# A tuned two-block kernel: lighter pair loop, reordered late units and an interleaved seam to the first FFN

## The reference

```python
h = rms_norm(x, pre_g)
conv_in, z_c, u_s, z_s, g_c, g_s = split(h @ w_in)
cu = ca * sigmoid(cb)                      # conv_in = (ca, cb)
cu = silu(layer_norm(causal_depthwise_conv(cu, conv_w, conv_b)))   # 31 taps
conv_out = (cu * silu(z_c)) @ w_conv_out
y = gelu(s5_mimo(u_s, ...))                # 32 groups, complex state of 64, scan over time
y = y * sigmoid(y @ w_glu + b_glu)
ssm_out = (y * silu(z_s)) @ w_ssm_out
merged = sigmoid(g_c) * conv_out + sigmoid(g_s) * ssm_out
x = x + rms_norm(merged @ w_out, post_g)
```

## Time and profile before

| | us |
|---|---|
| median of 3 runs (2633.86 to 2638.43) | 2634.6 |
| the profiled execution | 2629.72 |
| its span, first to last instruction | 2627.9 |

### The profile page before, as it was taken

One profiled execution on the slowest core, in us unless ns is written; L12 is line 12 of the kernel. 1 busy time (PEld: TensorE's weight loads), 2 busy tenths in 40 slices (PEclk: granted clock), 3 DMA queues, 4 the chain that ended last, 5 costly groups with the idle time before them and its releaser, 6 DMA issues.

```text
span 2627.9 us, 36163 instructions
## 1 busy us (share of the span) xinstructions
PE 2536.4 (97%) x13941; PEld 1951.4 (74%) x13941; DVE 1269.8 (48%) x1578; ACT 853.8 (32%) x1152; POOL 1197.5 (46%) x601
## 2 busy tenths in 40 slices
PE   8999999899999999888999999999999999999999
PEld 7666668678888776876788887888887446788887
DVE  7999775543322478566433322333225665433301
ACT  5422253432222335233322223322223233322221
POOL 4799834444444446212444444444443201444443
PEclk9999999899999999999999999999999999999999
DMA  5222213233333322002333333333333211333332
GB/s 147 73 72 67 72 55 112 64 96 94 90 90 96 104 81 61 20 3 66 91 96 89 90 96 93 95 96 90 90 96 87 59 33 33 92 92 96 94 91 80
DMA packets 417608, 212.85 MB, mean 81 GB/s; under 512 B 16774, under 2 KB 415932, under 8 KB 417500
## 3 DMA queue, kind: packets, MB, share of 16 engines
q1 hardware_dynamic: 414475, 209.05, 27.5%
q10 hardware_dynamic: 3024, 2.30, 0.4%
HBM read 209.22 MB, written 2.10 MB: 80 GB/s over the span
## 4 chain that ended last, share of the span: by engine, by line
PE 85%; POOL 7%; DVE 5%; ACT 1%; issue 1%; DMA 0%; ACTq 0%; POOLq 0%; DVEq 0%
PE bank L339 22%; PE bank L336 22%; PE bank L332 22%; PE bank L1314 3%; POOL w_lo L312 2%; PE bank L1316 2%; PE bank L1315 2%; PE bank L2097 2%; PE bank L2659 1%; PE bank L2658 1%; PE bank L2701 1%; PE bank L2617 1%; POOL tmp L767 1%; POOL tmp L772 1%; POOL tmp L761 1%
## 5 line engine op out<-in xcount | busy, mean ns | idle before, releaser
L312 POOL TENSOR_TENSOR w_lo<-w_raw,w_hi 128x1024 fp32r<-128x1024 f32 (+3 forms) x420 | 979.3, 2332 | 1316.7 <-ACT w_hi L303 1314.9
L303 ACT ACTIVATE w_hi<-w_raw 128x1024 fp32r<-128x1024 f32 (+3 forms) x420 | 424.8, 1012 | 1395.6 <-PE bank L339 1208.3
L332 PE MATMUL bank<-hH,w_hi 128*128 128x512 f32 x1728 | 451.7, 402 | 18.3 <-ACT w_hi L303 8.9
L336 PE MATMUL bank<-hL,w_hi 128*128 128x512 f32 x1728 | 440.9, 396 | 1.6 <-DVE hL L358 1.6
L339 PE MATMUL bank<-hH,w_lo 128*128 128x512 f32 x1728 | 438.0, 395 | 0.0
L332 PEld LDWEIGHTS bank<-hH,w_hi 128*128 128x128 f32 x1728 | 326.0, 189 | 110.6 <-ACT w_hi L303 11.4
L336 PEld LDWEIGHTS bank<-hL,w_hi 128*128 128x128 f32 x1728 | 325.3, 188 | 83.1 <-DVE hL L358 3.8
L339 PEld LDWEIGHTS bank<-hH,w_lo 128*128 128x128 f32 x1728 | 323.9, 187 | 79.1
L504 DVE TENSOR_TENSOR tmp<-bank,R 128x512 f32<-128x512 f32 x88 | 60.8, 691 | 400.4 <-PE bank L339 400.2
L510 DVE TENSOR_TENSOR ffn_aL<-tmp,ffn_aH 128x512 f32 (+1 forms) x88 | 156.0, 1773 | 86.2 <-ACT ffn_aH L473 86.2
L336 PE MATMUL bank<-ffn_aL,w_hi 128*128 128x512 f32 x704 | 179.8, 395 | 0.0
(11 more groups left out here) (482 smaller groups left out, 2755.5 us busy)
## 6 DMA issues: line engine op xcount, KB each, us to landing
w_raw<-in_ffn_w_gate SPq DMA_DIRECT2D x88, 512.0 KB, 3.8
w_raw<-in_ffn_w_up SPq DMA_DIRECT2D x88, 512.0 KB, 3.8
w_raw<-in_ffn_w_down SPq DMA_DIRECT2D x64, 512.0 KB, 3.7
w_raw<-in_w_in SPq DMA_DIRECT2D x48, 512.0 KB, 3.8
w_raw<-in_even_w_in SPq DMA_DIRECT2D x26, 512.0 KB, 3.8
w_raw<-in_ffn_w_down SPq DMA_DIRECT2D x32, 384.0 KB, 3.2
w_raw<-in_w_conv_out SPq DMA_DIRECT2D x8, 512.0 KB, 3.6
w_raw<-in_w_out SPq DMA_DIRECT2D x8, 512.0 KB, 3.6
```

Of the source, the lines that this page charges most:

```text
L303: nc.scalar.activation(w_hi[u % 2][:, 0:K, :], w_raw[u % 4][:, 0:K, :], ACT.Identity).then_inc(w_hi_ready, 1)
L312: nc.gpsimd.tensor_tensor(w_lo[u % 2][:, 0:K, :], w_raw[u % 4][:, 0:K, :], w_hi[u % 2][:, 0:K, :].bitcast(F32), ALU.subtract).then_inc(w_l ...
L332: nc.tensor.matmul(out, H[:, k, :], sH[:, k0 + k, :], start=start and k == 0, stop=False)
L336: nc.tensor.matmul(out, H[:, k, :], sL[:, k0 + k, :], start=False, stop=False)
```

## The change

Its diff, cut to what it does:

- `phases` on GpSimd makes only `ph_sin`; `tables` on ScalarE takes `Abs` of it, its sine, and as cosine the sine of a quarter turn less the absolute value. The memory for `ph_cos` and `quarter` goes.
- The loop has 11 taps per pair instead of 12; 16 more come after it. Every pair has 2 units; `LATE_UNITS` has 6. Four late units come ahead of `cs(14)`, two behind it.
- `y_rest` of all tiles comes behind the last tap; the gate units use banks 6 and 7 instead of 2 and 3, with waits that fit.
- `first_unit` has the order of `unit`: high pass (waits for `w_hi`), low pass, then the pass of `w_lo` (waits for it only there).
- GpSimd's subtraction for the second FFN unit waits for the diagonal tiles. VectorE adds tile 7 too, and its `hL` steps come behind all scalings and additions.
- The first FFN begins with `first_two`: units 0 and 1 share each slice as it comes. Unit 2 follows, then the norm's product, then unit 3. ScalarE converts unit 2's weights ahead of its last square.

```diff
@@ order of units @@
-                mine = [gates.pop(0) for _ in range(3 if i >= PAIRS - 2 else 2)]
+                mine = [gates.pop(0) for _ in range(2)]
...
-        LATE_UNITS = list(range(len(ROLE), len(ROLE) + 4))
-        ROLE += gates[:4]
+        LATE_UNITS = list(range(len(ROLE), len(ROLE) + 6))
+        ROLE += gates[:6]
@@ first FFN, TensorE @@
+        def first_two(pe, u, q):
...
+            for k in range(DT):
+                pe.wait_ge(h_hi, DT * q + k + 1)
+                for c in range(2):
+                    nc.tensor.matmul(bank_of(u + c)[:, :], w_hi[(u + c) % 2][:, k, :], hH[:, k, :], start=k == 0, stop=False)
+            for k in range(DT):
+                pe.wait_ge(h_lo, DT * q + k + 1)
+                for c in range(2):
+                    nc.tensor.matmul(bank_of(u + c)[:, :], w_hi[(u + c) % 2][:, k, :], hL[:, k, :], start=False, stop=False)
+            for c in range(2):
+                pe.wait_ge(w_lo_ready, u + c + 1)
+                for k in range(DT):
+                    ins = nc.tensor.matmul(bank_of(u + c)[:, :], w_lo[(u + c) % 2][:, k, :], hH[:, k, :], start=False, stop=k == DT - 1)
+                ins.then_inc(unit_done, 1)
...
-            for c in range(2):
+            if e == 0:
+                first_two(pe, U, q)
+            for c in range(0 if e else 2, 2):
                 unit(pe, U + c, 8, hH, hL, ready=(h_lo, DT * q) if c == 0 else None)
+            if e == 0:
+                unit(pe, U + 2, 8, hH, hL)
             norm_pe(pe)
-            for c in range(2, 4):
+            for c in range(2 if e else 3, 4):
@@ first FFN, ScalarE @@
                 for j in range(DT):
+                    if j == 7:
+                        split_hi(act, U + 2)
...
-                split_hi(act, u + 2, it, 4)
+                if not (first and e == 0):
+                    split_hi(act, u + 2, it, 4)
@@ block 1, GpSimd @@
-                g.tensor_tensor(ph_cos[p_][:, :], ph_sin[p_][:, :], quarter[:, 0:1].to_broadcast([P, T]), ALU.add).then_inc(ph_ready, 1)
...
-                if len(PAIR_UNITS[i]) > 2:
-                    split_lo(pool, u0 + 3)
...
-            for n_ in range(U_GLU, U_F[0] + (2 if STOP > U_F[0] else 0)):
+            for n_ in range(LATE_UNITS[4], U_F[0] + (1 if STOP > U_F[0] else 0)):
                 split_lo(pool, n_)
+            pool.wait_ge(ln_gated, DIAG + TT)
+            if STOP > U_F[0]:
+                split_lo(pool, U_F[0] + 1)
@@ block 1, ScalarE @@
+                s.activation(cosT[p_][:, :], ph_sin[p_][:, :], ACT.Abs, scale=TURN_TO_RAD / TURN).then_inc(act_step, 1)
+                turned = act_sent(act_step)
                 s.activation(sinT[p_][:, :], ph_sin[p_][:, :], ACT.Sin, scale=TURN_TO_RAD / TURN).then_inc(tab_ready, 1)
-                s.activation(cosT[p_][:, :], ph_cos[p_][:, :], ACT.Sin, scale=TURN_TO_RAD / TURN).then_inc(tab_ready, 1)
+                act.wait_ge(act_step, turned)
+                s.activation(cosT[p_][:, :], cosT[p_][:, :], ACT.Sin, scale=-1.0, bias=QUARTER).then_inc(tab_ready, 1)
...
-            y_split(3, gelu(3))
             after_unit(LATE_UNITS[2])
             after_unit(LATE_UNITS[3])
+            y_split(3, gelu(3))
+            after_unit(LATE_UNITS[4])
+            after_unit(LATE_UNITS[5])
@@ block 1, VectorE @@
-        X_BY_DVE = (1, 3, 6)
+        X_BY_DVE = (1, 3, 6, 7)
...
-                taps(3)
+                taps(2)
...
-            taps(16)
-            for j in range(3):
-                y_rest(j)
+            taps(28)
             y_out(3)
             taps(len(TAP_ORDER) - taps_sent[0])
-            y_rest(3)
+            for j in range(4):
+                y_rest(j)
...
+            for j in range(DT):
+                o_scale(j)
+                if j in X_BY_DVE:
+                    x_add(j)
+            for j in range(DT):
                 norm_lo(j)
@@ block 1, TensorE @@
-                pe.wait_ge(w_lo_ready, u + 1)
+                pe.wait_ge(w_hi_ready, u + 1)
                 H, L = w_hi[u % 2], w_lo[u % 2]
                 for k in range(K):
                     if ready:
+                        pe.wait_ge(h1_hi if ready[0] is h1_lo else y_hi, ready[1] + k + 1)
+                    mm(out[:, :], H[:, k, :], sH[:, k, :], start=k == 0, stop=False)
+                for k in range(K):
+                    if ready:
                         pe.wait_ge(ready[0], ready[1] + k + 1)
-                    mm(out[:, :], H[:, k, :], sH[:, k, :], start=k == 0, stop=False)
                     mm(out[:, :], H[:, k, :], sL[:, k, :], start=False, stop=False)
+                pe.wait_ge(w_lo_ready, u + 1)
+                for k in range(K):
                     ins = mm(out[:, :], L[:, k, :], sH[:, k, :], start=False, stop=k == K - 1)
...
             w_in_unit(LATE_UNITS[0])
-            w_in_unit(LATE_UNITS[1])
+            for c in range(1, 4):
+                w_in_unit(LATE_UNITS[c])
             cs(PAIRS - 2)
-            w_in_unit(LATE_UNITS[2])
-            w_in_unit(LATE_UNITS[3])
+            w_in_unit(LATE_UNITS[4])
+            w_in_unit(LATE_UNITS[5])
```

More of the change, by code:

```diff
@@ L593, in build @@
         ph_sin = [b.put(f"ph_sin{i}", [P, T], I32) for i in range(3)]
-        ph_cos = [b.put(f"ph_cos{i}", [P, T], I32) for i in range(3)]
         b = Map(tab_at)
@@ L954, in first_act @@
             silu(0)
-            silu(1)
             after_unit(U_GC)
-            for j in range(2, 5):
+            for j in range(1, 5):
                 silu(j)
@@ L2841, in constants @@
     small[:, 4] = np.where(i % 64 < 32, -1.0, 1.0)
+    small[:, 5] = np.pi / 2
     s, t = i[:, None], i[None, :]
```

38 lines of the change are left out of this document (14 added, 24 removed).

## The result

The changed kernel takes 2613.4 us (median of 4 runs, 2608.2 to 2613.95), the kernel before 2634.2 us in the runs beside it (4 runs, 2632.92 to 2638.43). The ratio is 0.9914, with a 95% interval of 0.9903 to 0.9926: 20.8 us faster. The predicted number was 2610.6 us, range 2605.5 to 2620. The sign, the range and most terms held; the number is 2.8 us too low, and that small difference hides two larger ones, which this part takes apart.

A forecast was written before the change was run, and what follows sets the result against it. TensorE, busy 97% of the span, was held by waits and slow clock, GpSimd setting the pair loop's 14.84 us period. Terms summed to 24.0 us: 2629.7 to 2605.7 profiled, plus 4.9 to the median, 2610.6 us; range 2605.5 to 2620.

The forecast's parts named there:

- loop (pair 3 to the end of its units): Pair loop: waits 15.0, two slow stretches 3.4 and refills 1.5 go, less 0.5 for lag; gain 19.4 us.
- unit 0 in the new order: Kernel start: all high products run first, so unit 0 ends at 22.9 instead of 21.5 us; cost 1.4 us.
- input product of pair 0 (`Abs` ahead of the `u_s` copies): At tables(0): `Abs` delays the `u_s` copies in ScalarE's queue; cost 0 to 0.63, taken as 0.5 us.
- last state product: Behind the pair loop: the 2.7 us wait for `s_im` and 1.5 us of clock loss go; gain 4.2 us.
- `w_ssm_out`, output product's first unit: Late block 1: 1.0 us gained as the wait for `w_lo` goes; 1.0 us lost waiting for high tile and `mL`.
- seam, up to the fifth unit's end: Block 1's end into the first FFN: fifth unit starts at 536.0 instead of 538.36 us; gain 2.3 us.
- cover of 3.7 us: Pair loop: the new order asks for `w_lo` 3.7 us later, covering GpSimd's lag of some 3 us by pair 15.
- Rival A: Pair loop: GpSimd stays the bound and slow stretches move; total gain near 16 us, 2618.5 us; chance 0.21.
- both slow stretches go: Pair loop: without waits the two stretches at 0.83 clock, 1.7 us each, vanish; gain 3.4 us.
- Rival D: Phase-to-table ring becomes the loop's bound if `Abs` adds table loads; slower, 2641 us at 15.5 us per pair; chance 0.03.
- Rival C: Behind the loop: deferred taps and `y_rest` hold the column means, 7 us go; 2617.5 us; chance 0.08.
- The first diagonal: End of block 1: the diagonal tile no longer runs beside GpSimd's subtraction, falling from 1632 to under 300 ns; gain 1.36 us.

The follow-up runs named there:

- after_again: The changed kernel, unchanged, run and profiled a second time; 2612.4 us, ratio 0.9916.
- fifth_early: The changed kernel with ScalarE converting the fifth FFN unit's weights right behind the norm's root; 2607.8 us, ratio 0.99.
- old_seam: The changed kernel with the seam between block 1 and the first FFN as in the kernel before; 2614.9 us, ratio 0.9925.
- best_mix: fifth_early plus slice-by-slice order in unit 0 and the output product's first unit, and last `u_s` copies ahead of the next weights; 2601.9 us, ratio 0.9875.
- both shifted ones: after_shift1 and after_shift2, the changed kernel with added norm products ahead of the second block's mixer; 2611.0 and 2614.5 us.
- twelve_taps: The changed kernel with 12 taps per pair again and 12 instead of 28 between loop and `y_out(3)`; 2616.3 us, ratio 0.9926.
- order_only: The kernel before with only the new product order in `first_unit`; 2633.5 us, ratio 0.9995.
- before_again: The kernel before, unchanged, run and profiled a second time; 2635.1 us (one run).
- one_phase: The kernel before with only the lighter phase step: one GpSimd phase product per pair, `Abs` on ScalarE; 2620.75 us, ratio 0.9954.
- before_shift1: The kernel before with the norm's product ahead of the second block's mixer done three times, 0.9 us added; 2639.1 us (one run).
- after_shift1: The changed kernel with the norm's product ahead of the second block's mixer done three times, 0.9 us added; 2611.0 us (one run).
- after_shift2: The changed kernel with the norm's product ahead of the second block's mixer done five times, 1.8 us added; 2614.5 us (one run).

## Why the prediction was right, and where it was off

The terms against the milestones of the table:

| term | forecast | measured |
|---|---|---|
| loop (pair 3 to the end of its units) | 19.4 | 19.5 |
| unit 0 in the new order | -1.4 | -1.5 |
| input product of pair 0 (`Abs` ahead of the `u_s` copies) | -0.5 | -0.3 |
| pair 0 to pair 3, net, with the slow stretch from 70 us | not foreseen | -1.2 |
| last state product | 4.2 | 4.25 |
| `w_ssm_out`, output product's first unit | 1.0 - 1.0 | 0.2 |
| seam, up to the fifth unit's end | 2.3 | about 2.0 |
| sum up to 560 us | 24.0 | 23 |
| stage of small products | 0 | -7.9 (3 of it luck of before) |

**Loop.** The bound was read rightly. The two needs worked out from before's rows were 13.72 (GpSimd) and 13.5 (TensorE), and TensorE's pair came out at 13.56. GpSimd's own step, pair by pair, is its phase product:

```profile
109.16 1.04 POOL L775 TENSOR_TENSOR ph_sin<-tidx,phase 128x512 int32<-128x512 int32 x1
...
273.81 1.04 POOL L775 TENSOR_TENSOR ph_sin<-tidx,phase 128x512 int32<-128x512 int32 x1
```

These are 12 pairs, (273.81 - 109.16) / 12 = 13.72 us each, just the need that was worked out. So GpSimd is still the slowest of the three and falls behind TensorE by 0.16 us per pair; over 16 pairs that is 2.6 us, which the later demand for `w_lo` covers, as argued: no wait but one of 0.3 us in 80 to 305 us. By this estimate the cover of 3.7 us would not last in a loop of twice the pairs. The group of all its phase steps:

```profile
L775 POOL TENSOR_TENSOR ph_sin<-tidx,phase 128x512 int32<-128x512 int32 x14 | 14.6, 1042 | 1.1
```

One product of 1.04 us remains, the second, of the earlier trace rows, is gone. Rival A (2618.5 us) falls with this.

**The clock in the loop.** The choice that both slow stretches go, worth 3.4 us, was right here: none of the kernels with the changed loop shows one between 80 and 340 us (after, after_again, fifth_early, old_seam, best_mix, both shifted ones, and twelve_taps too, although it waits 5.5 us in short pieces). order_only shows one at 290 to 300 us (0.71), before_again three. The Trainium skill, "TensorE: Matmul & The Clock Gate", Part 1: The HAM clock gate, with activity releasing a slow default, agrees as far as the loop goes. That twelve_taps keeps its clock in spite of waits of up to 1.2 us, while the kernel before lost it behind some waits of 1.6 us and not behind others, and not behind its longest one in the loop, of 2.6 us at 290.7 us, no row here explains.

**Table loads.** Rival D needed loads in every pair. The rows of ScalarE in 80 to 305 us:

```profile
L883 ACT ACTIVATE cosT<-ph_sin 128x512 f32<-128x512 int32 x15 | 9.5, 631 | 48.1 <-POOL ph_sin L775 48.1
...
L885 ACT ACT_TABLE_LOAD x2 | 2.6, 1283 | 0.0
```

Fifteen `Abs`, and two loads at the line of the sine, as many as before; over 60 to 330 us the kernel before, the changed one, one_phase, order_only and twelve_taps load seven times each. At 631 ns the `Abs` cost what the sine row said. The rule of the Trainium skill, "ScalarE: Activation LUTs", Table sets: the hidden batching unit, that `abs` is in every set, agrees with this.

**Last state product and deferred work.** The 4.2 us came (stage 6.09 us, now 1.84). Rival C wanted the taps to hold the column means: they end at 323.1 us, the means start at 324.34, with 1.2 us to spare; that is tight, and the `y_rest` steps took 4.9 us, not the 8 the rival allowed.

**The start.** Unit 0 ended at 23.00 us, forecast 22.9:

```profile
15.76 3.67 PE L1330 MATMUL bank<-hH,w_hi 128*128 128x512 f32 x8 [0.95 <-DVE hL L1034]
19.27 2.03 PE L1334 MATMUL bank<-hL,w_hi 128*128 128x512 f32 x8
21.13 2.04 PE L1337 MATMUL bank<-hH,w_lo 128*128 128x512 f32 x8
```

At tables(0) `Abs` was costed as a delay (0.5 us; 0.3 measured), and that held. What the sum did not have is the slow stretch from 70 us, which is deeper than before, 0.66 against 0.83, and takes a further 1.2 us by pair 3: the clock was weighed at the waits that go and at the new one at the fifth unit, but not at one that stays. It is tempting to put this on the longer wait for `u_s` (3.4 us, before 3.2), but the runs speak against it. The window from 70 us of one_phase, which has `Abs` and the 3.4 us wait, and of before_shift1, which has neither:

```profile
70.00:80.00 10.00, 8.69 (x30) 6.41 (x31) 9.97 (x15) 1.26 (x3) 2.73 (x2) 0.83 0.18 52
...
70.00:80.00 10.00, 9.68 (x28) 6.66 (x29) 9.37 (x15) 0.18 (x1) 2.78 (x3) 0.66 0.18 52
```

From the input product of pair 0 to that of pair 3 the executions with 0.83 there (before, before_again, one_phase, best_mix) take 38.9 us, all others 39.8 to 40.5. So the loss goes with the deeper stretch, which came with and without the change; what decides its depth stays open, and best_mix, which has 2.5 us of wait and 0.83, is one execution too few to settle it.

**The seam.** Its steps came out close, the sum closer than its steps:

```profile
L1286 DVE TENSOR_SCALAR tmp<-ident,rowst x4: 281/282/286, 476.9 to 477.4; 128x128 f32<-128x128 f32 x4
...
477.81 2.34 POOL L312 TENSOR_TENSOR w_lo<-w_raw,w_hi 128x1024 fp32r<-128x1024 f32 x1 [5.94 <-DVE tmp L1286]
...
479.07 1.28 DVE L1290 TENSOR_TENSOR oT<-oT,bank 128x512 f32<-128x512 f32 x2 [1.35 <-PE bank L1494]
...
488.12 1.95 ACT L473 ACTIVATE hH<-xT,par 128x512 fp32r<-128x512 f32 x3 [0.97 <-POOL xT L828]
```

The first diagonal takes 286 ns or less instead of 1632, with the subtraction behind it: 1.6 us gained (forecast 1.36). Four more profiles with the old order there (before_again, order_only, one_phase, old_seam) show 1628 to 1632 ns, and four more with the new one (after_again, twelve_taps, fifth_early, best_mix) 286 ns at most. The last `hH` is done at 488.12 + 1.95 = 490.07 us, 11.0 us after 479.07 (forecast 11.3). The norm's product, counted from the end of `w_out`, came 0.7 us earlier than before where 0.5 later was forecast: the two interleaved units gave more. The fifth unit then gained 3.6 us over `w_out`'s end, not 2.3, waited 2.54 us (forecast 3), and lost 1.7 us to the slow stretch from 515 us, which the prediction named ("would take 1.5 of it") and did not put into the sum. Together about 2.0, and old_seam gives about the same by its own way.

**From the sum to the number.** Here the prediction was right partly by cancellation. It added to its profiled 2605.7 us the 4.9 us between profile and median of before. The changed kernel's profiled execution took 2613.09 and its median is 2613.4, so no such difference exists for it. The 7.4 us by which the profiled time was missed are the 7.9 us of the small-products stage, less the few tenths by which the part ahead of it did better than the sum; about 3 of them are the same luck of before's profile. The second profiles, before_again against after_again, show what a less quick execution of before makes of it: 25.2 us gained at the norm's product ahead of the mixer (899.45 against 874.23), 28.0 where the small-products stage begins, 5.2 lost in it, 22.8 at the end. So the mechanism of the loop and the seam was right, and that the number came within 2.8 us is in part luck: a stage that nobody costed took back about 5 us, and clock stretches elsewhere gave some of it.

## What to carry to other kernels

Where three engines are nearly full, work out each one's need per round from its own time line, and take load off the one with the highest until the matmul engine no longer waits (here GpSimd stayed 0.16 us per pair behind, within its cover); asking later for a result buys slack once and moves the wait to the next result of the same engine. Where a new order is good for the loop, give the first unit, which has to wait for its inputs slice by slice, its own order. And look at the ScalarE queue ahead of each new wait: a weight conversion moved ahead of a table load and a silu took away a wait of 2.5 us and had the kernel 3.2 to 3.7 us ahead at 871 us, more than the whole rebuilt seam.

## What the runs showed of the hardware

The stage of small 64 by 64 products took from 170.3 to 178.5 us for identical instructions, at a granted clock of 0.98 to 0.93; one execution of the changed kernel with 0.9 us of added work 135 us earlier had it 4.5 us shorter, at 0.96. So a difference of up to 0.3% between two versions of such a kernel can come from a place that neither touches. Second, a VectorE step of 128 by 128 elements that takes 273 to 286 ns alone took 1632 ns when it started beside a GpSimd subtraction, and ended with it (1628 to 1632 ns in five profiles); a single wait put the two in order. Third, waits of the same length are not followed by the same clock: the 2.5 us wait ahead of the fifth unit was followed by five microseconds at 0.66 in after and by 1.00 in twelve_taps, after_shift1 and after_shift2; the 3.2 us wait for `u_s` by ten microseconds at 0.83 in before and at 0.66 in before_shift1.
